# Scaling expert rows by gathered gate rows before the adding scatter, and copying the outputs from DRAM to DRAM

## What is computed

```
x = x + g1 * mix
h = rms_norm(x, p["norm2_g"]) * (1 + sc2) + sh2
x = x + g2 * grouped_moe(h, ...)          # g2: one row of 1024 per request (9 requests)

for e in range(N_EXPERTS):                # 16 experts, each token uses 2 of them
    hidden = silu(hf @ w_gate[e]) * (hf @ w_up[e])
    y = y + gates[:, e:e + 1] * (hidden @ w_down[e])
```

## Time and profile before

| what | value |
|---|---|
| median of 3 runs | 1188.93 us (1186.75 to 1189.68) |
| the profiled execution | 1187.63 us, its span 1185.8 us |
| PE busy | 1068.2 us, 90% of the span |
| DVE, ACT, POOL busy | 389.4, 244.0, 143.5 us |
| mean granted TensorE clock | 0.96 |
| DMA over the span | 217.05 MB, mean 183 GB/s |
| chain that ended last | PE 79%, DVE 8%, DMA 5%, ACT 4%, issue 3% |

### The profile page before, as it was taken

One profiled execution on the slowest core, in us unless ns is written; L12 is line 12 of the kernel. 1 busy time (PEld: TensorE's weight loads), 2 busy tenths in 40 slices (PEclk: granted clock), 3 DMA queues, 4 the chain that ended last, 5 costly groups with the idle time before them and its releaser, 6 DMA issues.

```text
span 1185.8 us, 21577 instructions
## 1 busy us (share of the span) xinstructions
PE 1068.2 (90%) x8635; PEld 714.0 (60%) x8635; DVE 389.4 (33%) x894; ACT 244.0 (21%) x486; POOL 143.5 (12%) x218
## 2 busy tenths in 40 slices
PE   5899999989979979889999999955999999999991
PEld 4445764456745757667677754425676767677770
DVE  2100738956777655200000003353111111111114
ACT  4111232127745335200000001121111101010100
POOL 0000210110000000200000010010222222222221
PEclk9999999999979989999999999976999999999996
DMA  9542855345000248880030027066796996999935
GB/s 344 221 149 88 311 170 189 110 122 193 1 1 1 72 144 283 231 232 1 19 123 1 1 99 293 36 220 223 256 305 204 358 366 215 316 381 373 382 93 195
DMA packets 103029, 217.05 MB, mean 183 GB/s; under 512 B 9477, under 2 KB 17749, under 8 KB 102694
## 3 DMA queue, kind: packets, MB, share of 16 engines
q1 hardware_dynamic: 91446, 184.42, 43.5%
q0 software_dynamic: 11504, 31.52, 9.8%
HBM read 196.87 MB, written 19.05 MB: 182 GB/s over the span
## 4 chain that ended last, share of the span: by engine, by line
PE 79%; DVE 8%; DMA 5%; ACT 4%; issue 3%; SPq 0%; DVEq 0%; POOL 0%; ACTq 0%; POOLq 0%
PE ps L2105 17%; PE ps L1996 10%; PE ps L1651 10%; PE ps L2116 9%; PE ps L2007 6%; PE ps L2051 4%; PE ps L1677 3%; PE ps L1696 3%; PE ps L1595 3%; PE ps L1625 2%; DMA mem<-in_w_branch_b 2%; DMA mem<-in_x_sample 2%; PE ps L1778 2%; PE ps L2110 1%; ACT mem L952 1%
## 5 line engine op out<-in xcount | busy, mean ns | idle before, releaser
L2105 PEld LDWEIGHTS ps<-mem 128*64 128x64 f32 x3584 | 198.5, 138 | 24.8 <-issue 21.4
L2105 PE MATMUL ps<-mem 128*64 128x128 f32 x3584 | 209.5, 275 | 2.1 <-DVE mem L1552 0.9
L1996 PE MATMUL ps<-mem 128*128 128x320 f32 x512 | 139.2, 433 | 1.1 <-DVEq L1359 1.1
L1996 PEld LDWEIGHTS ps<-mem 128*128 128x128 f32 x512 | 97.3, 190 | 41.5 <-issue 1.3
L1651 PE MATMUL ps<-mem 128*128 128x512 f32 (+1 forms) x320 | 113.3, 514 | 1.8 <-ACT mem L912 0.9
L2116 PE MATMUL ps<-mem 128*64 128x512 f32 x448 | 107.1, 597 | 4.2 <-DVE mem L1566 0.5
L1651 PEld LDWEIGHTS ps<-mem 128*128 128x128 f32 x320 | 54.2, 191 | 58.5 <-issue 58.5
L1595 PE MATMUL ps<-mem 128*128 128x128 f32 x432 | 66.9, 294 | 22.8 <-DVE mem L1129 8.8
L1397 DVE TENSOR_TENSOR mem<-mem,ps 128x320 f32<-128x320 f32 x32 | 15.6, 488 | 198.1 <-PE ps L2007 198.1
L1564 DVE TENSOR_TENSOR mem<-mem,ps 128x128 f32<-128x128 f32 x56 | 16.1, 288 | 186.9 <-PE ps L2105 186.9
L1595 PEld LDWEIGHTS ps<-mem 128*128 128x128 f32 x432 | 53.4, 151 | 36.7 <-DVE mem L1129 9.8
(11 more groups left out here) (288 smaller groups left out, 1141.3 us busy)
## 6 DMA issues: line engine op xcount, KB each, us to landing
mem<-in_w_exp_gate SPq DMA_DIRECT2D x16, 2048.0 KB, 12.5
mem<-in_w_exp_up SPq DMA_DIRECT2D x16, 2048.0 KB, 17.9
mem<-in_w_exp_down SPq DMA_DIRECT2D x16, 2048.0 KB, 22.3
mem<-in_w_ada SPq DMA_DIRECT2D x12, 2048.0 KB, 14.4
mem<-in_w_in SPq DMA_DIRECT2D x9, 2048.0 KB, 13.1
mem<-in_cache_b_k SPq DMA_DIRECT2D x8, 1024.0 KB, 5.6
mem<-in_cache_b_v SPq DMA_DIRECT2D x8, 1024.0 KB, 8.5
mem<-in_w_out SPq DMA_DIRECT2D x2, 2048.0 KB, 11.4
```

The lines of the kernel that those rows point to most:

```text
L1996: last = mm(b[:, 0:320], w[:, k, P * (m % 4):P * (m % 4) + P], hT[:, k, 320 * h:320 * h + 320], start=(k == 0), stop=(k == KD - 1))
L2105: last = mm(b[UNIT * h:UNIT * h + UNIT, 0:P], x_, w[:, k, 256 * h + P * c:256 * h + P * c + P], start=(k == 0), stop=(k == KD - 1), skip_g ...
```

## The change

The gate `g2` moves from behind the sum over experts to in front of it: each unit's rows are multiplied by the routing weight and by the gate rows of their requests, and are then added onto `yd`, which holds the first residual `x1` from the start instead of zeros. What `yd` holds at the end is the output, and it is copied to the output tensors from DRAM to DRAM.

- `yd` is no longer zeroed, but for 64 spare rows. POOL stores `x1` into it, 5 tiles of 512 KB, in the place where it spread `g2` (9 DMAs).
- POOL stores the adaLN parts 0 to 3 in `modd` too (4 DMAs), so that each row of it may be gathered.
- DVE works out, for each unit and partition, which half row of `modd` holds the gate (7 small operations, two of them without a wait between).
- For each unit POOL gathers those half rows (`gather_scale`): a copy of the numbers and an indirect DMA of 128 rows of 2 KB into the one buffer `g2_rows`. It stands between the wait for `yj` of unit `u` and the scatter of unit `u`, and loads the rows for unit `u + 1`.
- `yj` is made by DVE in place of ACT, at the end of DVE's unit, and waits for `down_full`, `y_st` and `g2_ld`. `down_used` is then told by DVE, and ACT tells `gate_used` right behind its second Silu.
- The loads, DVE's ten operations and the stores at the end are replaced by 5 DMAs of 512 KB from `yd` to the outputs.

```diff
             sp.wait_ge(y_all, 1)
             for t in range(NT):
-                sp.dma_start(ysum[t], yd[P * t:P * t + P, :]).then_inc(tile_ld[t], 16)
-            for t in range(NT):
-                sp.wait_ge(e_out, 100 + t + 1)
-                sp.dma_start(out_rows("y", t), ysum[t]).then_inc(out_st, 16)
+                sp.dma_start(out_rows("y", t), yd[P * t:P * t + P, :]).then_inc(out_st, 16)
...
-                    for r_ in range(0, TOK + UNIT, P):
-                        n_ = min(P, TOK + UNIT - r_)
-                        pool.dma_start(yd[r_:r_ + n_, :], zeros[0:n_]).then_inc(zeros_st, 16)
+                    pool.dma_start(yd[TOK:TOK + UNIT, :], zeros[0:UNIT]).then_inc(zeros_st, 16)
...
+            pool.wait_ge(m9_first, 4)
+            dst = modd[:, 0:2048].rearrange("c (i j n) -> j c i n", i=4, j=4)
+            for j in range(4):
+                pool.dma_start(dst[j], m9[32 * j:32 * j + NCOND, 0:4, :]).then_inc(mod_st, 16)
             ada_rows(pool, 4, 4, m9_st[1])
...
-            pool.wait_ge(h2_ready, 2 * NT)
-            spread(pool, g2, 5120, 1024, g2_ld)
+            for t in range(NT):
+                pool.dma_start(yd[P * t:P * t + P, :], x1[:, t, :]).then_inc(x1_st, 16)
...
+            def gather_scale(u, n):
+
+                g.tensor_copy(idx_g2, cond_row[:, u]).then_inc(idx_g2_ready, 1)
+                hold(idx_g2_ready, n)
+                pool.indirect_dma_start(g2_rows, None, mod_halves,
+                                        bass.IndirectOffsetOnAxis(ap=idx_g2, axis=0)).then_inc(g2_ld, 16)
...
                     hold(yj_ready, u + 1)
+                    gather_scale(bass.ds(u + 1, 1), u + 2)
                     g.tensor_copy(idx_out, ids[:, bass.ds(u, 1), 1:2].rearrange("p j a -> p (j a)")).then_inc(idx_out_ready, 1)
...
-                    hold(down_full, u + 1)
-                    hold(y_st, u * 16 + 16)
-                    s.activation(yj, bank(7), ACT.Copy, scale=unit_w[:, bass.ds(u, 1)]).then_inc(yj_ready, 1)
                 act.sem_inc(gate_used, 1)
-                act.sem_inc(down_used, 1)
...
                     turn_x()
+                    hold(down_full, u + 1)
+                    hold(y_st, u * 16 + 16)
+                    hold(g2_ld, u * 16 + 16)
+                    v.scalar_tensor_tensor(yj, bank(7), unit_w[:, bass.ds(u, 1)], g2_rows, ALU.mult, ALU.mult).then_inc(yj_ready, 1)
                 dve.sem_inc(up_used, 1)
+                dve.sem_inc(down_used, 1)
```

More of the change, by code:

```diff
@@ L312, in build @@
         dest, slot_token = view(O_TMP + 1280, UNITS), view(O_TMP + 1280 + UNITS, UNITS)
+        cond_f, cond_i = view(O_TMP + 1280 + 2 * UNITS, UNITS), view(O_TMP + 1280 + 3 * UNITS, UNITS).bitcast(I32)
+        g2_rows = view(O_TMP + 2048, HALF)
+        cond_row = view(O_TMP + 2048 + HALF, UNITS + TOK // UNIT + 2).bitcast(U32)
+        idx_g2 = view(O_TMP + 2048 + HALF + UNITS + TOK // UNIT + 2, 1).bitcast(U32)
         cnt = view(rt + 80, 16); nt = view(rt + 96, 16)
@@ L349, in build @@
         h2_halves, y_halves = (r.rearrange("r (h n) -> (r h) n", h=2) for r in (h2d, yd))
+        mod_halves = modd.rearrange("c (h n) -> (c h) n", n=HALF)
         rows2 = {n: (o[i].rearrange("l b s h d -> (l b s) (h d)"), o[j].rearrange("l b s h d -> (l b s) (h d)"))
@@ L570, in build @@
         later_ready = sem("later_ready")
+        mod_st, x1_st, idx_g2_ready, cond_ready = sem("mod_st"), sem("x1_st"), sem("idx_g2_ready"), sem("cond_ready")
         lgs_ready = sem("lgs_ready")
@@ L775, in gather @@
                                         bass.IndirectOffsetOnAxis(ap=idx_in, axis=0)).then_inc(hx_ld, 16)
-            pool.wait_ge(zeros_st, 96)
+            def gather_scale(u, n):
[3 more added lines that the diff above has]
+                                        bass.IndirectOffsetOnAxis(ap=idx_g2, axis=0)).then_inc(g2_ld, 16)
             gather(slice(0, 1), 1)
@@ L780, in _ @@
             gather(slice(1, 2), 2)
+            pool.wait_ge(cond_ready, 1)
+            pool.wait_ge(mod_st, 64)
+            pool.wait_ge(m9_st[0], 64)
+            gather_scale(slice(0, 1), 1)
+            pool.wait_ge(x1_st, 16 * NT)
+            pool.wait_ge(zeros_st, 16)
             for e in range(NE):
@@ L794, in _ @@
             hold(hx_ld, (at + n) * 16 + 32)
+            hold(g2_ld, (at + n) * 16 + 16)
             pool.sem_inc(y_all, 1)
@@ L898, in _ @@
             act.wait_ge(ro_st[1], 64)
-            act.wait_ge(zeros_st, 96)
+            act.wait_ge(zeros_st, 16)
             for h in range(IH):
@@ L1543, in _ @@
             dve.sem_inc(weights_ready, 1)
+            step(v.tensor_scalar(cond_f, slot_token, 2.0 * (SEQ - DEC_S), 0.0, ALU.subtract, ALU.max))
+            step(v.tensor_copy(cond_i, cond_f))
+            step(v.tensor_scalar(cond_i, cond_i, (2 * DEC_S).bit_length() - 1, None, ALU.logical_shift_right))
+            step(v.tensor_copy(cond_f, cond_i))
+            step(v.tensor_scalar(cond_f, cond_f, 12.0, 10.0, ALU.mult, ALU.add))
+            own(v.memset(cond_row[:, UNITS:UNITS + 2], 0))
+            own(v.tensor_scalar(cond_row[:, 0:UNITS], cond_f, row_half, None, ALU.add))
+            own.settle()
+            dve.sem_inc(cond_ready, 1)
             r = result(dve, "slot_w")
```

## The result

The changed kernel took 1198.58 us (median of 6 runs, 1193.79 to 1198.87) beside 1187.73 us of the kernel before on the same chip (6 runs): a ratio of 1.0074 on record, with a 95% interval of 1.0055 to 1.0093 (the two medians alone give 1.0091), 0.7% slower. I had forecast 1188.0, no change that can be told; the measured time lies inside the whole range that I gave, 1180 to 1203, and outside the 1184.5 to 1191.5 of the forecast itself. It came out near where the first rival had put it, at 1196.4, though that rival's cause carries only a part of it.

The account below looks back on a forecast made before the run. PE, busy 332.3 of 338 us, was taken to bound the units, with the end following once PE is done. End -6.7 and units +6.3 made -0.4 against 1187.63: 1187.2, given as 1188.0; range 1180 to 1203.

Parts of the forecast that it names:

- first rival: In the units: the scatter waits behind the gather, long-stretch landings each 0.5 us later; sum +8.8, 1196.4 us; chance 0.28.
- The end: Behind the last scatter's landing: 10.1 us against 19.1, 9.0 us less (4.3 to 10.6).
- third rival: At the end: the DRAM copy runs at half rate, 12.7 us instead of 8.0; sum +4.3, 1191.9 us; chance 0.07.
- The later scatter at the end: Last scatter: POOL's added copy, wait and gather, and DVE's slower operation, start it 2.3 us later.
- The ring's fixed part: In the units, from yj over the scatter back to yj: 4.4 us a turn without the landing.
- Units: +6.3 us: Over all units: yj falling behind costs 4.0 us and later landings 2.3, together 6.3 us more (0 to 27).
- I take 0.1 us for each of the 23 landings: Long stretches of units: the gather makes each scatter's landing 0.1 us later, 2.3 us in all.
- the same bytes in smaller bursts, which can shorten landings: Weight loads in the units: asking for the gate part half a unit sooner may shorten landings; no cost counted.
- 3.3 us of room: In a unit: yj may start 3.3 us later before PE has to wait for DVE's next first product.
- each short landing was to win back the whole room of 3.3 us: Between the long stretches: two landings of 4.9 us win everything back, each turn 2.8 us under a unit.

Follow-up runs that it names:

- e4: The change with gate_used told by DVE together with up_used and down_used, so the gate part is asked for late; 1187.93 us, ratio 0.9994.
- e12: e11 with two copies at the end, 2 MB and 512 KB, instead of five of 512 KB; 1185.25 us, ratio 0.9968.
- e9: e5 with the gate part asked for late, as in e4; 1182.34 us, ratio 0.9949.
- e5: The change with the loop's gather replaced by a POOL memset of 128x1792 elements, full delay without the gather's bytes; 1188.43 us, ratio 0.9994.
- e6: The change with the gather behind the scatter and the gate part late (e1 and e4 together); 1182.99 us, ratio 0.9959.
- e1: The change with the gather of gate rows moved behind the scatter on POOL, same instructions and bytes; 1183.94 us, ratio 0.9958.
- e8: The kernel before with the gate part asked for early, DVE telling gate_used together with up_used; 1189.02 us, ratio 0.9995.
- e11: e6 with the copy of the scatter's indices ahead of POOL's wait for yj; 1182.13 us, ratio 0.9949.
- e10: The change with both index copies ahead of POOL's wait for yj, gather, bytes and early gate part kept; 1183.68 us, ratio 0.9975.
- e2: The change without the gather in the loop over units, only unit 0's gate rows being gathered; 1180.88 us, ratio 0.9923.

## Why the prediction was wrong

- **The end** was right in mechanism and size. I had 0.3 + 8.0 + 1.4 + 0.4 = 10.1 us behind the last landing, and measured 0.4 + 10.0 + 0.4 = 10.8 (11.1 to 12.3 in the other profiles). The Trainium skill ("DMA: Bandwidth & Descriptors", latency and other measured facts) has 214 GB/s per direction as the full rate of copies between HBM tensors, measured on tiles of 128 rows with a padded row pitch. The rows of this copy, whose rows lie one behind the other, don't agree, and they decide here: four copies, 2.10 MB, landed in the 5.9 us between the first landing and the last, an estimate of 355 GB/s. So the third rival fell.
- **The later scatter at the end**, +2.3 us, measured +2.5: right.
- **The ring's fixed part**, 4.4 us from one `yj` to the next without the landing: 3.97 to the scatter and 0.35 from landing to `yj`, 4.3: right. That `yj` would wait for the landing in the long stretches, and PE then for DVE's product, came as written.
- **The step that failed is "Units: +6.3 us"**, and in it three parts. First, "I take 0.1 us for each of the 23 landings": over the long landings the mean went from 8.32 to 8.67, 0.35 more, and the first rival decided "from 0.3 us a landing on". Second, the sentence on `gate_used`, "the same bytes in smaller bursts, which can shorten landings", was costed at nothing with a gain in view. It went the other way: e4 gives back 0.8% by undoing only that. With the gate part late the units were 5.1 us longer than before, near the 6.3. Third, "3.3 us of room": I took it from the timeline of one unit inside an expert. At a change of expert DVE needs 1.3 us between `yj` and the next first product, where the forecast had left 0.2, so the room there is 2.2 us. The group of that product's line over the units of the kernel after shows it as time in which DVE waits for nothing:

```profile
L1588 DVE TENSOR_TENSOR mem<-mem,ps 128x128 f32<-128x128 f32 x56 | 16.1, 287 | 85.9 <-PE ps L2129 72.7 <-issue 13.2
```

  13.2 us in ten places, all changes of expert, and PE's six waits for a product of `hid` stand at six of them. Inside an expert the product follows `yj` at once, and PE waited for none. A smaller slip of the same sum: each short landing was to win back the whole room of 3.3 us, but 12.1 - 9.3 is 2.8, which is 1.0 us too little for the two.
- **A term that was missing** is the clock. In the unit of the timeline above and in the one from 935.4 us on, PE waited 2.96 and 2.83 us, and as it resumed the granted clock fell to 0.50 (1.2 GHz, the lower of its two levels) before it was back at 1.00. The busy times by stretch of the kernel after (the clock is the third figure from the end) show the wait, what followed it, and the rest of that unit; then both units whole, and two units without such a wait:

```profile
1029.50:1032.40 2.90, 0.02 (x1) 0.00 (x0) 1.04 (x2) 0.28 (x1) 0.62 (x2) 1.00 0.31 47
1032.60:1035.90 3.30, 3.30 (x31) 3.13 (x32) 0.29 (x1) 0.00 (x0) 2.13 (x3) 0.50 0.94 342
1036.00:1041.00 5.00, 4.65 (x29) 1.68 (x25) 1.27 (x3) 0.00 (x0) 1.19 (x2) 1.00 1.06 366
...
935.40:951.80 16.40, 13.39 (x150) 10.44 (x152) 2.60 (x6) 0.55 (x2) 3.76 (x6) 0.90 1.05 367
1024.00:1041.00 17.00, 13.64 (x152) 10.30 (x152) 2.60 (x6) 0.55 (x2) 4.30 (x7) 0.90 0.85 270
...
964.00:988.00 24.00, 23.69 (x304) 17.88 (x306) 5.11 (x12) 1.11 (x4) 8.21 (x13) 1.00 0.91 299
```

  The 0.90 of a whole unit is the mean of both levels. The 3.52 us for 32 matmuls above belong here; the same 32 took 1.97 in a unit of e12. In these two units PE was busy for 13.39 and 13.64 us, against 23.69 / 2 = 11.85 in each of the two without a wait: 3.3 of the 4.75 us more. So a wait of some 3 us cost about half as much again. Most of the other 1.4 us lies in the first unit, where the clock stood at 0.50 for 6.0 us from the start of the units, and before the change for 3.6; that stretch ran from 2.9 to 6.0 us in the profiles of the repaired and the other kernels, so it isn't put down to the change.
- **The first rival** had the right size, but its cause carries only a part of it. In e4 the gather still goes just ahead of the scatter in the same queue, and the long landings take 8.19 us, against 8.32 before and 8.11 in e9 without the gather. By the rule that I had put beside it (the Trainium skill, "DMA: Bandwidth & Descriptors", queues, rings and completion order), an engine takes the gather's descriptors ahead of the scatter's. By these rows such an order makes the landing 0.1 us longer with the gate part late (e9, e4) and 0.2 with it early (8.46 in e5, 8.67 in the change). More comes from the early gate part: 0.35 us without the gather (e9, e5) and 0.48 with it (e4, the change). Where the ring has room it adds next to nothing: 8.44 and 8.51 (e6, e1), 8.32 and 8.35 (before, e8). Why it lengthens the landings in the tight ring stays open: these are means of one profile each, the profile doesn't show single packets of a scatter, and e11 has 8.55 with the gate part late, without any harm.

What is shown: e1 and e10 leave the gather and its bytes in place, shorten only the ring, and the loss gives way to a gain (0.9958 and 0.9975). So it belongs to the ring as a whole and not to a part of it. The unit takes 12.1 us. The ring's fixed part and the mean long landing are 4.32 + 8.67 = 13.0 in the change, 4.13 + 8.46 = 12.6 in e5, 4.32 + 8.19 = 12.5 in e4 and 4.13 + 8.11 = 12.2 in e9; the units took 15.1, 4.4, 5.1 and 2.8 us more than before. In e10, with the landings of the change for its own, which its profile doesn't have, it is 3.16 + 8.67 = 11.8, an estimate, and under the unit. The forecast stood close to that edge, where a few tenths of a landing decide.

## What to carry to other kernels

When a change adds serial time to a ring that an asynchronous transfer closes, compare the ring with the unit's period first: far below it, added time cost next to nothing here (e1, e2); above it, each unit falls behind by the excess, and once the room is used up PE pays for it. Take the room at the tightest place (here the change of expert), not in a typical unit, and count the clock that PE may lose after a long wait. Then look for what may stand outside the ring: here two copies of indices, or the order of a gather and a scatter, were worth about 1%. An increment that lets a load start earlier is not free where the load runs beside a transfer that a tight ring waits for (0.8% in e4); where the ring had room, it cost nothing (e6, e8).

## What the hardware showed unexpectedly

- A copy from DRAM to DRAM ran at about 355 GB/s (worked out above), not far from the 412 of one-way loads and stores, and neither two queues (12.3 us from the last landing to the end) nor two larger copies (11.4) changed its time beyond the 10.8 to 12.3 of the other runs. Its first 512 KB landed 4.1 us after the issue, a store's 2.7.
- The 0.8 us between a copy of indices and the indirect DMA was not all a wait for the copy. In e11 the copy lies ahead of the wait for `yj`, and the scatter still starts 0.82 us behind `yj`'s end (1.57 - 0.75).
- The granted clock fell to 0.50 behind PE's waits of 2.83 and 2.96 us in the change, and behind the one of 2.4 us for weights in e12 (0.50 from 1141.8 to 1145.1 us), and rose to 1.00 again while PE was busy. Behind the shorter waits (up to 1.56 us in the change, 1.0 in e4, 1.2 in e5) it stayed at 1.00.
